# Attention on one core: the probabilities are normalised on GpSimd, and the transposed tile is copied and split in two halves, a PSUM bank each

## The reference

```
def attention(q, k, v):
    ...
    def one_block(qi):
        s = jnp.einsum('bqhgd,bshd->bhgqs', qi, k).astype(jnp.float32)
        p = jax.nn.softmax(s, axis=-1).astype(v.dtype)
        return jnp.einsum('bhgqs,bshd->bqhgd', p, v)
```

## Time and profile before

| | us |
|---|---|
| median of 3 runs | 2241.17 (2239.71 to 2244.13) |
| profiled execution, its own time | 2242.06 |
| its span in the profile | 2240.3 |
| attention of layer 0, about | 161 to 274 |
| attention of layer 1, about | 1424 to 1521 |

### The profile page before, as it was taken

How to read it: one execution, slowest core, us unless ns; L and a number is a source line. 1 busy time by engine, 2 the same in 40 slices (tenths; PEclk the granted TensorE clock), 3 DMA queues, 4 the chain that set the end, 5 groups by cost and what they waited for, 6 DMA issues and landing times.

```text
span 2240.3 us, 27947 instructions
## 1 busy us (share of the span) xinstructions
PE 2134.7 (95%) x11302; PEld 1807.4 (81%) x11302; DVE 1337.7 (60%) x1812; ACT 794.9 (35%) x1154; POOL 783.3 (35%) x359
## 2 busy tenths in 40 slices
PE   6889899999999999999999987899999999999997
PEld 6777788888888888888888876677867877888885
DVE  6459899856774587847616674798954353101113
ACT  2446711142324522223212344572234344222223
POOL 3220023232334433423323345103444555444442
PEclk9999999999999999999999989999999999999998
DMA  7110012123344134534323221102222332323321
GB/s 295 38 47 1 1 52 70 43 88 112 105 159 151 58 119 134 187 101 135 105 85 111 94 95 66 48 1 66 88 78 90 108 123 82 97 94 95 94 85 66
DMA packets 63200, 205.24 MB, mean 92 GB/s; under 512 B 7136, under 2 KB 8288, under 8 KB 62816
## 3 DMA queue, kind: packets, MB, share of 16 engines
q1 hardware_dynamic: 57744, 190.87, 26.2%
q10 hardware_dynamic: 5328, 12.59, 1.5%
HBM read 197.79 MB, written 5.64 MB: 91 GB/s over the span
## 4 chain that ended last, share of the span: by engine, by line
PE 78%; DVE 17%; ACT 2%; issue 1%; DMA 1%; POOL 1%; ACTq 0%; DVEq 0%
PE ps L529 70%; DVE conv_acc L1624 3%; DVE ps L1624 2%; DVE unit_stats L1585 2%; PE ps L555 2%; DVE pt1l L1605 1%; DVE probs L1599 1%; DVE pt0l L1605 1%; PE ps L736 1%; PE ps L592 1%; PE ps L573 1%; PE ps L613 1%; PE ps L583 1%; PE ps L757 1%; PE ps L600 1%
## 5 line engine op out<-in xcount | busy, mean ns | idle before, releaser
L425 POOL TENSOR_TENSOR w_l<-w_raw,w_h 128x1024 fp32r<-128x1024 f32 (+3 forms) x296 | 683.7, 2314 | 1305.7 <-ACT w_h L893 1305.4
L529 PE MATMUL ps<-h_h,w_h 128*128 128x512 f32 (+1 forms) x1296 | 430.4, 372 | 5.9 <-ACT t L1145 4.2
L529 PE MATMUL ps<-h_l,w_h 128*128 128x512 f32 (+1 forms) x1296 | 426.1, 369 | 0.0
L529 PE MATMUL ps<-h_h,w_l 128*128 128x512 f32 (+1 forms) x1296 | 425.3, 368 | 0.0
L893 ACT ACTIVATE w_h<-w_raw 128x1024 fp32r<-128x1024 f32 (+3 forms) x296 | 280.5, 950 | 212.2 <-PE ps L529 148.6
L529 PEld LDWEIGHTS ps<-h_h,w_h 128*128 128x128 f32 x1296 | 244.8, 190 | 55.8 <-ACT t L1145 6.6
L529 PEld LDWEIGHTS ps<-h_h,w_l 128*128 128x128 f32 x1296 | 245.7, 190 | 43.6
L529 PEld LDWEIGHTS ps<-h_l,w_h 128*128 128x128 f32 x1296 | 245.4, 189 | 42.9 <-issue 1.2
L1485 DVE CUSTOM_DVE_ANT_0 ps<-ada_raw,c_row 128x1024 f32<-128x1024 f32 x160 | 268.4, 1677 | 9.1 <-DMA ada_raw<-in_ada 4.1
L529 PE MATMUL ps<-f_h,w_h 128*128 128x258 f32 (+1 forms) x672 | 173.1, 339 | 0.9 <-DVE t L1810 0.9
L529 PE MATMUL ps<-f_h,w_l 128*128 128x258 f32 (+1 forms) x672 | 173.5, 340 | 0.0
(11 more groups left out here) (236 smaller groups left out, 3222.6 us busy)
## 6 DMA issues: line engine op xcount, KB each, us to landing
w_raw<-in_w SPq DMA_DIRECT2D x222, 512.0 KB, 3.6
ada_raw<-in_ada SPq DMA_DIRECT2D x80, 512.0 KB, 3.6
w_raw<-in_w SPq DMA_DIRECT2D x50, 256.0 KB, 3.2
ada_first<-in_ada SPq DMA_DIRECT2D x16, 512.0 KB, 6.7
w_raw<-in_w SPq DMA_DIRECT2D x16, 384.0 KB, 3.1
x<-in_x ACTq DMA_DIRECT2D x8, 384.0 KB, 17.6
x_again<-in_x ACTq DMA_DIRECT2D x8, 384.0 KB, 7.7
x_between<-x SPq DMA_DIRECT2D x8, 384.0 KB, 2.3
```

What stands on the lines that cost most here:

```text
L425: nc.gpsimd.tensor_tensor(wl[:, s % RING, 0:n], raw[:, s % RAW, 0:n], wh[:, s % RING, 0:n], ALU.subtract).then_inc(split, 1)
L529: ins = nc.tensor.matmul(at(out, c0, c1), w[:, s % RING, b * P:(b + 1) * P], m[:, kt, first + c0:first + c1], start=(kt == 0 and n == 0), ...
```

## The change

The multiplication of step 4 moves to GpSimd: VectorE computes only the reciprocal and raises `recip`; a new function `probabilities` in GpSimd's list waits for it and multiplies, and the transposes wait for GpSimd. Region `B` becomes two halves, each at the start of its own PSUM bank (`half_from`): the key tiles 0 to 2 and 3 to 5, and in a short unit one query tile each. ScalarE's copy, VectorE's subtraction and the release of the bank go half by half, so that each unit has two copies and two subtractions of half the size. The transposes of half p of a unit wait for the subtraction of half p of the unit before. The number of matmuls and transposes is the same.

```
+            if q_tiles(unit) == 1:
+                return [3 * part + k for k in range(3)]
+            return [2 * part + k for k in range(2)]
...
+            c = 2048 + 512 * part
+            return psf[:, c:c + P * len(half_tiles(unit, part))].rearrange("p (k q) -> p k q", q=P)
...
+            def probabilities(ly):
+
+                for u, (h, q0, nk, q, nq, b) in enumerate(units(ly)):
+                    n, c = q_tiles((h, q0, nk, q, nq, b)), 2 * (u % 8)
+                    pool.wait_ge(*seen("recip", ly, u))
+                    for r in range(n):
+                        p_r = pr[:, u % 2, r * nk:(r + 1) * nk]
+                        nc.gpsimd.tensor_scalar(p_r, p_r, ust[:, 3, c + r:c + r + 1], None, ALU.mult).then_inc(
+                            *(pool_norm.up("normed", ly, u) if r == n - 1 else pool_norm.up()))
...
+                split_run(at_s, ly * SLABS + S_CONV + 1 + RING)
+                at_s = ly * SLABS + S_CONV + 1 + RING
+                probabilities(ly)
...
-                    take("B", "pt", ly, u)
                     pe.wait_ge(*seen("normed", ly, u))
-                    for k in range(nk * q_tiles(us[u]) // P):
-                        ins = nc.tensor.transpose(at(B, k * P, (k + 1) * P), pr[:, u % 2, k * P:(k + 1) * P], ident)
-                    ins.then_inc(*pe_done.up("pt", ly, u))
+                    if u == 0:
+                        take("B", "pt", ly, len(us) - 1, 1)
+                    for part in range(2):
+                        if u:
+                            pe.wait_ge(*seen("free", "pt", ly, u - 1, part))
+                        for i, k in enumerate(half_tiles(us[u], part)):
+                            ins = nc.tensor.transpose(half_from(us[u], part)[:, i, :], pr[:, u % 2, k * P:(k + 1) * P],
+                                                      ident)
+                        ins.then_inc(*pe_done.up("pt", ly, u, part))
...
-                        act.wait_ge(*seen("pt", ly, u - 1))
...
-                        ph = pt(b)[0]
-                        nc.scalar.activation(key_rows(ph, us[u - 1]),
-                                             by_key_tile(at(B, 0, nk * q_tiles(us[u - 1])), us[u - 1]),
-                                             ACT.Copy).then_inc(*act_hi.up("pth", ly, u - 1))
+                        for part in range(2):
+                            act.wait_ge(*seen("pt", ly, u - 1, part))
+                            nc.scalar.activation(half_to(pt(b)[0], us[u - 1], part), half_from(us[u - 1], part),
+                                                 ACT.Copy).then_inc(*act_hi.up("pth", ly, u - 1, part))
...
-                        link(v.reciprocal(ust[:, 3, c:c + n], ust[:, 2, c:c + n]), dve_tmp)
-                        for r in range(n):
-                            p_r = pr[:, (u - 1) % 2, r * nk:(r + 1) * nk]
-                            v.tensor_scalar(p_r, p_r, ust[:, 3, c + r:c + r + 1], None, ALU.mult).then_inc(
-                                *(dve_tmp.up("normed", ly, u - 1) if r == n - 1 else dve_tmp.up()))
+                        v.reciprocal(ust[:, 3, c:c + n], ust[:, 2, c:c + n]).then_inc(*dve_tmp.up("recip", ly, u - 1))
...
+                        for part in range(2):
+                            dve.wait_ge(*seen("pth", ly, u - 2, part))
+                            v.tensor_tensor(half_to(pl, us[u - 2], part), half_from(us[u - 2], part),
+                                            half_to(ph, us[u - 2], part), ALU.subtract).then_inc(
+                                *dve_lo.up("free", "pt", ly, u - 2, part))
```

More of the change, by code:

```diff
@@ L326, in by_key_tile, with half_tiles, half_from, half_to @@
             return ap.rearrange("p (r k q) -> p k r q", k=CTX // P, q=P)
+        def half_tiles(unit, part):
+            if q_tiles(unit) == 1:
+                return [3 * part + k for k in range(3)]
+            return [2 * part + k for k in range(2)]
+        def half_from(unit, part):
+            c = 2048 + 512 * part
+            return psf[:, c:c + P * len(half_tiles(unit, part))].rearrange("p (k q) -> p k q", q=P)
+        def half_to(ap, unit, part):
+            if q_tiles(unit) == 1:
+                return key_rows(ap, unit)[:, 3 * part:3 * part + 3, :]
+            return ap[:, 0:CTX // P, part * P:(part + 1) * P]
         def key_rows(ap, unit):
@@ L749, in values @@
                             pe.wait_ge(*seen("tile", ly, "v"))
-                        pe.wait_ge(*seen("free", "pt", ly, u))
+                        pe.wait_ge(*seen("free", "pt", ly, u, 1))
                     ph, pl = pt(b)
@@ L1071, in _ @@
                         if u >= 2:
-                            act.wait_ge(*seen("pt", ly, u - 2))
+                            act.wait_ge(*seen("pt", ly, u - 2, 1))
                         n, c = q_tiles(us[u]), 2 * (u % 8)
@@ L1595, in _ @@
                         dve.wait_ge(*seen("free", "scores", ly, u - 1))
-                        link(v.reciprocal(ust[:, 3, c:c + n], ust[:, 2, c:c + n]), dve_tmp)
-                        for r in range(n):
-                            p_r = pr[:, (u - 1) % 2, r * nk:(r + 1) * nk]
-                            v.tensor_scalar(p_r, p_r, ust[:, 3, c + r:c + r + 1], None, ALU.mult).then_inc(
-                                *(dve_tmp.up("normed", ly, u - 1) if r == n - 1 else dve_tmp.up()))
+                        v.reciprocal(ust[:, 3, c:c + n], ust[:, 2, c:c + n]).then_inc(*dve_tmp.up("recip", ly, u - 1))
                     if u >= 2:
                         h, q0, nk, q, nq, b = us[u - 2]
-                        dve.wait_ge(*seen("pth", ly, u - 2))
                         ph, pl = pt(b)
[L1605 to L1608, removed]
+                        for part in range(2):
[3 more added lines that the diff above has]
+                                *dve_lo.up("free", "pt", ly, u - 2, part))
                 for j in range(BR):
```

## The result

The changed kernel takes 2263.93 us (median of 4, 2263.54 to 2266.24) against 2240.44 for the kernel before on the same chip: ratio 1.0104, 95% interval 1.0086 to 1.0121, so 1.0% slower. 0.5% faster was forecast, and the range ended at 2250.

The account below looks back on a forecast made before the run. The prediction took VectorE's list to bound layer 1 attention and waits over region `B` layer 0; savings of 5.4 us in layer 1 and 6.9 in layer 0 gave -12.3, so 2229 us for the median, range 2217 to 2250.

Parts of the forecast that it names:

- What bounds the kernel: Layer 1 attention before the change: the chain never leaves VectorE, 2.77 us a unit.
- The loop: Attention: one turn from transposes through scores, reciprocal and multiplication back, in two units, 3.98 us plus the multiplication.
- X: Time of GpSimd's multiplication of 128x768 in attention: taken as 1.22 us; 1.04 to 1.45 had chance 0.40.
- T: Time of an attention unit after the change: 1.99 + X/2, or 2.5 us if more; 2.60 in layer 1.
- My own sign: Profile after: GpSimd rows of 1.6 us or longer mean wrong by size; units longer than 1.99 + X/2, by loop.
- The halves: Two half-size subtractions and copies per long unit in attention: VectorE 0.14 us more, ScalarE 0.17 more.
- TensorE's floor: Rival in attention: with X below about 1.04, TensorE's 2.5 us a unit decides; 2220 to 2221 us; chance 0.22.
- Contention: Attention: VectorE's negation waits for GpSimd's end, but comes some 2.3 us after the reciprocal; costed at nothing.
- 0.2 us for the short unit: Layer 0 attention: added per head since the short unit's two exponentials delay ScalarE's next copy; guess between nothing and 0.4.

Follow-up runs that it names:

- the deeper pipeline: Changed kernel with a third buffer for the probabilities and transposes, copies, subtractions and value matmuls one unit later: 2213.28 us, ratio 0.9868 to the kernel before.
- GpSimd alone: Kernel before with GpSimd multiplying, the region kept whole with one copy and one subtraction: 2275.36 us, ratio 1.0151 to the kernel before.
- the reciprocal first: Changed kernel with VectorE taking the reciprocal of unit u-1 ahead of the row maximum of u: 2235.79 us, ratio 0.9969 to the kernel before.

## Why the prediction was wrong

**What bounds the kernel: right,** for layer 1. With VectorE's list as the bound, the halves leave 2.72 us and when the multiplication is taken away and its new place is hidden (the deeper pipeline), a unit falls to 2.40.

**The loop: right.** Worked out as 1.99 + X/2 per unit. Four runs with X of 0.83, 1.25, 1.47 and 2.21 us and halved region gave 2.42, 2.65, 2.75 and 3.13. Between 1.25 and 2.21 the slope is 0.48 / 0.96 = 0.5; at 0.83 the formula and TensorE's list meet, both at about 2.4.

**X: this is the step that failed.** The prediction bounded it from above "by GpSimd's own two-input instruction of that shape, 1.81" and took the middle, 1.22, since one input halves what is fetched. It is 2.21, outside both ends. The bound rested on the belief that fewer inputs can't be slower, and no row bore that out. It was not even firm for two inputs: in the trace of before, GpSimd's two-input rows of 128x768 run from 1.54 us (`f_l` at 769.05) to 2.79 (`norm_tmp` at 19.97, beside VectorE's work). Put into the prediction's own sums, 2.21 gives T = 3.10 and +10.4 us in layer 1, (19.0 + 8.8 + 1.9) / 2 + 0.2 = 15.05 per head and +11.9 in layer 0, together 2263.5: measured 2263.93. So the whole miss is this one term. I had written that X "could exceed 1.81", with a chance of about 0.12 for what lies beyond the range, and let the range end there all the same. My own sign held: rows of 1.6 us or longer, so wrong by its size and not by its loop.

**The halves: mis-sized.** I charged VectorE 0.14 us a unit and ScalarE 0.17. VectorE's chain pays nothing, as the two subtractions overlap, and alone the halves make the kernel 0.3% faster. With GpSimd multiplying they are worth about 0.5%, the distance between GpSimd alone and the changed kernel. Neither price entered my sum, for the loop that I added up passes neither copy nor subtraction.

**TensorE's floor: right in kind,** 2.40 to 2.42 instead of 2.5.

**Contention: dismissed rightly, for a reason only half true.** I counted on the negation falling outside GpSimd's instruction. At nine units, the short ones above all, it fell inside, and took 0.16 us all the same, because it came 1.76 us or more after GpSimd's start. The Trainium skill, "SBUF — State Buffer", section "Who interferes with whom", lets a VectorE instruction with two SBUF inputs contend with any GpSimd instruction that reads SBUF; this case agrees. That they block each other for a whole instruction, as the prediction has it, this case shows for GpSimd's instructions with two tensors (1.35 us beside a slab, 0.51 and 0.67 beside the multiplication) and not for the one with a single tensor, which is clear after about 0.75 of its 2.21 us; there the measurement decides. One SBUF input in place of two is no safeguard by itself: in the trace of before, VectorE's copy of 512 columns at 1524.93 (`conv_in`) took 2.57 us beside a slab and 0.42 without one, at 281.31.

**Layer 0:** its 0.2 us for the short unit was not needed. With 2.21 the bare formula gives 14.85 and 14.95 was measured.

What stays open: why GpSimd's multiplication by one factor is dearer than one by a repeated second tensor. The prices are measured; what happens inside GpSimd was not. Nor was the deeper pipeline run with the region whole, so how much of its 1.3% needs the halves is not known.

## What to carry to other kernels

Work moved to a slower engine is free as long as every loop of waits that passes it, divided by the units that it spans, stays under the longest list of an engine. So add up the loop, not the busy times, and before the move shorten the loop or give it one more buffer and one more stage of distance. Here the same 2.21 us cost 1.0% with two buffers and gained 1.3% with three, and with two buffers and the reciprocal first they gained 0.3%. Take the price of an operation on an engine from a row of that very operation: a bound from another one, even one with more inputs, can lie on the wrong side.

## What the runs showed of the hardware that was not expected

- GpSimd, 128x768 fp32 in SBUF: copy 0.83 us, product with a repeated second tensor 1.47, product with a constant 2.13, with a factor per partition 2.21.
- VectorE's small negation with two SBUF inputs waits for the end of a GpSimd instruction with two tensors (1.35 us beside a slab, 0.51 and 0.67 beside the product with a repeated tensor). Beside GpSimd's product with one factor it is held only at the start: 0.38 us when it begins 0.53 us after GpSimd, 0.21 at 0.70, and 0.16 from 0.79 on.
- Two VectorE subtractions of 384 columns without a wait between them take 0.93 us of the chain, as one of 768; each alone lasts 0.55.
